# Memory keys and values as four weight stages, the values computed with tokens in partitions

## What is computed

```python
X_HEADS, X_HEAD_DIM, MEM_LEN = 4, 128, 256

def rmsnorm(x, g):
    return x * lax.rsqrt(jnp.mean(x * x, axis=-1, keepdims=True) + NORM_EPS) * g

def memory_cross_attn(xq, mem_kv):          # mem_kv = rmsnorm(memory, g) @ w_mem_kv[layer]: 256 x 1024
    q = xq.reshape(bsz, t, X_HEADS, X_HEAD_DIM)
    k, v = jnp.split(mem_kv, 2, axis=-1)
    ...
    s = jnp.einsum('bthd,bmhd->bhtm', q, k) * (X_HEAD_DIM ** -0.5)
    p = jax.nn.softmax(s, axis=-1)
    o = jnp.einsum('bhtm,bmhd->bthd', p, v)
```

## Time and profile before

| | |
|---|---|
| median of 3 runs | 2449.39 us (2448.02 to 2449.98) |
| the profiled execution, its time | 2450.39 us |
| its span, which the rows show | 2448.6 us |
| share of PE, PEld, DVE, ACT, POOL | 97%, 80%, 50%, 27%, 60% |
| mean clock granted to TensorE | 0.993 of full speed |

### The profile page before, as it was taken

How to read it: one execution, slowest core, us unless ns; L and a number is a source line. 1 busy time by engine, 2 the same in 40 slices (tenths; PEclk the granted TensorE clock), 3 DMA queues, 4 the chain that set the end, 5 groups by cost and what they waited for, 6 DMA issues and landing times.

```text
span 2448.6 us, 32730 instructions
## 1 busy us (share of the span) xinstructions
PE 2384.1 (97%) x12156; PEld 1964.8 (80%) x12156; DVE 1217.8 (50%) x2000; ACT 657.0 (27%) x1329; POOL 1457.1 (60%) x1461
## 2 busy tenths in 40 slices
PE   8999999999999999999999999999999989999997
PEld 6877778887888888787788888888888877888885
DVE  4335654334302325776358552055787874755402
ACT  3233321002201113455221110025666543111100
POOL 8654456666666667554458777661333355877761
PEclk9999999999999999999999999999999999999998
DMA  4222222222222322221222222222112212222221
GB/s 171 90 95 87 87 77 96 95 95 95 95 95 95 123 99 88 70 87 53 69 86 95 95 96 96 101 78 69 54 68 70 70 52 78 95 95 95 97 99 54
DMA packets 59762, 214.49 MB, mean 88 GB/s; under 512 B 6624, under 2 KB 6752, under 8 KB 59488
## 3 DMA queue, kind: packets, MB, share of 16 engines
q1 hardware_dynamic: 56880, 206.55, 24.9%
q10 hardware_dynamic: 2736, 5.96, 0.7%
HBM read 210.38 MB, written 2.10 MB: 87 GB/s over the span
## 4 chain that ended last, share of the span: by engine, by line
PE 84%; DVE 11%; ACT 3%; issue 1%; DMA 0%; POOL 0%; DVEq 0%; ACTq 0%; POOLq 0%
PE acc L556 23%; PE acc L558 23%; PE acc L557 22%; PE ps_s L699 3%; PE ps_o L727 2%; PE ps_t L713 2%; PE acc L768 1%; PE acc L770 1%; PE acc L769 1%; DVE hg_in L2085 1%; DVE hg_in L1633 1%; ACT w_hi L1462 1%; DVE hg_level_q L2133 1%; DVE hg_level_k L2133 1%; DVE ps_s L1589 1%
## 5 line engine op out<-in xcount | busy, mean ns | idle before, releaser
L513 POOL CAST w_hi<-w_raw 128x512 fp32r<-128x512 f32 x688 | 439.9, 668 | 714.8 <-DMA w_raw<-stream 714.6
L556 PE MATMUL acc<-h_hi,w_hi 128*128 128x512 f32 (+1 forms) x1844 | 723.0, 392 | 6.4 <-DVE h_lo L1555 2.9
L558 PE MATMUL acc<-h_hi,w_lo 128*128 128x512 f32 (+1 forms) x1844 | 706.2, 383 | 0.0
L557 PE MATMUL acc<-h_lo,w_hi 128*128 128x512 f32 (+1 forms) x1844 | 704.8, 382 | 0.0
L515 POOL TENSOR_TENSOR w_lo<-w_raw,w_hi 128x512 fp32r<-128x512 f32 x384 | 514.2, 1339 | 231.2 <-ACT w_hi L1462 231.2
L517 POOL TENSOR_TENSOR w_lo<-w_raw,w_hi 128x512 fp32r<-128x512 f32 x384 | 532.7, 1387 | 0.0
L556 PEld LDWEIGHTS acc<-h_hi,w_hi 128*128 128x128 f32 x1844 | 347.7, 189 | 73.7 <-DVE h_lo L1555 4.7
L558 PEld LDWEIGHTS acc<-h_hi,w_lo 128*128 128x128 f32 x1844 | 346.9, 188 | 69.4
L557 PEld LDWEIGHTS acc<-h_lo,w_hi 128*128 128x128 f32 x1844 | 347.8, 189 | 64.0 <-issue 0.5
L1611 DVE COPY y_all<-acc 128x512 f32<-128x512 f32 x31 | 21.4, 691 | 270.0 <-PE acc L558 238.5
L556 PE MATMUL acc<-hid_hi,w_hi 128*128 128x512 f32 x352 | 138.9, 395 | 0.0
(11 more groups left out here) (346 smaller groups left out, 3685.6 us busy)
## 6 DMA issues: line engine op xcount, KB each, us to landing
w_raw<-stream SPq DMA_DIRECT2D x384, 512.0 KB, 3.2
toeplitz<-ext_in ACTq DMA_DIRECT2D x16, 256.0 KB, 3.7
out<-x_res SPq DMA_DIRECT2D x4, 512.0 KB, 2.6
x_res<-x_in SPq DMA_DIRECT2D x3, 512.0 KB, 7.0
mem<-mem_in ACTq DMA_DIRECT2D x1, 1024.0 KB, 5.5
consts<-consts_in SPq DMA_DIRECT2D x1, 656.0 KB, 9.6
x_res<-x_in SPq DMA_DIRECT2D x2, 256.0 KB, 5.1
rope<-rope_in ACTq DMA_DIRECT2D x1, 512.0 KB, 6.6
```

The lines of the kernel that those rows point to most:

```text
L513: nc.gpsimd.tensor_copy(hi[:, half], raw[:, half]).then_inc(hi_made, 1)
L556: nc.tensor.matmul(ps, hi, x_hi[:, k, 0:cols], start=(k == 0), stop=False)
L557: nc.tensor.matmul(ps, hi, x_lo[:, k, 0:cols], start=False, stop=False)
L558: mm = nc.tensor.matmul(ps, lo, x_hi[:, k, 0:cols], start=False, stop=(k == st.kt - 1))
```

## The change

`memkv` becomes four stages: `memk0`, `memv0`, `memk1`, `memv1`, each four column blocks of eight tiles. The stream holds the same tiles; those of `memv0` and `memv1` are now in the lead order, four tiles of one feature tile side by side. The keys are computed as before (`memk0` by the lead steps in units 9 to 16, `memk1` in 13 units). The values are computed as the first stages of the kernel do it: a block of 128 memory tokens is stationary, and the 512 value columns of the layer are moving, in 16 steps of three matmuls spread over 12 units. Two banks hold a layer's values, one for each token block, tokens in partitions, and ScalarE copies each of them to `mem_v` with the scale 1/rms of its token, which now lies along the partitions. The eight turnings, VectorE's eight scaled copies to `normed` and its eight copies out of `ps_t` are gone. For the new scale, `both_norms` computes two more columns: VectorE first adds the two halves of `mem_sq` (one more addition of 128x256), one 256-column product gives the row as before, and two one-column products, with `mem_sq` stationary, give the sums with tokens in partitions. Root and reciprocal cover 258 columns where they covered 256.

```diff
+MEMORY = ["memk0", "memv0", "memk1", "memv1"]
-LEAD = {*TOKENS, "up0", "memkv", "a_in", ...
+LEAD = {*TOKENS, "up0", "memk0", "memv0", "memv1", "a_in", ...
-    ("a_in", 16, 8), ("memkv", 16, 8), ("a_out", 8, 12), ...
+    ("a_in", 16, 8), *[(name, BANKS, 8) for name in MEMORY], ("a_out", 8, 12), ...
...
-        for c in range(st.cbs):
+        for c in range(MEM // P if name.startswith("memv") else st.cbs):
...
+        mem_part = [("memv0", 12), ("memk1", 13), ("memv1", 12)]
+        mem_at = {name: MEM_FIRST + sum(units for _, units in mem_part[:i]) for i, (name, _) in enumerate(mem_part)}
+        mem_at["a_out"] = MEM_FIRST + sum(units for _, units in mem_part)
...
-                    for half in range(2):
-                        mm = nc.tensor.matmul(ps_t[:, 0:MEM], const("ones"), mem_sq[:, 0, half * MEM:(half + 1) * MEM],
-                                              start=(half == 0), stop=(half == 1))
+                    nc.tensor.matmul(ps_t[:, 0:MEM], const("ones"), mem_sq[:, 0, 0:MEM], start=True, stop=True)
+                    for b in range(MEM // P):
+                        mm = nc.tensor.matmul(ps_t[:, MEM + b:MEM + b + 1], mem_sq[:, 0, b * P:(b + 1) * P], const("ones")[:, 0:1],
+                                              start=True, stop=True)
...
+            def mem_values(st, first, end):
+                for i in range(first, end):
+                    k, b = divmod(i, MEM // P)
+                    slot = st.first_slot + k // 2
+                    if k == 0:
+                        bank_free(st, b)
+                    if k % 2 == 0 and b == 0:
+                        pe.wait_ge(split_made, slot + 1)
+                    hi, lo = (w[:, slot % RING, BANKS * (k % 2):BANKS * (k % 2 + 1), :].rearrange("p t n -> p (t n)") for w in (w_hi, w_lo))
+                    out_, cols = banks[st.banks[b]][:], slice(b * P, (b + 1) * P)
+                    nc.tensor.matmul(out_, h_hi[:, k, cols], hi, start=(k == 0), stop=False)
+                    nc.tensor.matmul(out_, h_lo[:, k, cols], hi, start=False, stop=False)
+                    mm = nc.tensor.matmul(out_, h_hi[:, k, cols], lo, start=False, stop=(k == st.kt - 1))
+                    if k % 2 and b == MEM // P - 1:
+                        mm.then_inc(slot_done, 1)
...
-            for c in range(BANKS, mem_st.cbs):
-                if c % 8 >= 4:
-                    also[mem_turn(c) + 1].append(lambda c=c: transpose_v(mem_st, c, normed[:, c % 2, :], MEM // P))
...
+            def take_memory(layer):
+                st_ = stages[f"memv{layer}"]
+                act.wait_ge(slot_done, st_.first_slot + st_.slots)
+                for b in range(MEM // P):
+                    nc.scalar.activation(mem_v[layer][:, b, :], banks[st_.banks[b]][:], ACT.Copy,
+                                         scale=small["rstd_mem"][:, MEM + b:MEM + b + 1]).then_inc(st_.free, 1)
...
+            also[mem_at["memk1"]] = lambda: take_memory(0)
+            also[mem_at["a_out"]] = lambda: take_memory(1)
...
+            step.wait()
+            step(nc.vector.tensor_tensor(mem_sq[:, 0, 0:MEM], mem_sq[:, 0, 0:MEM], mem_sq[:, 0, MEM:], ALU.add), x_total)
```

More of the change, by code:

```diff
@@ L59 @@
 WIDE = {"ffn_in0": (4, 5, 6), "ffn_in1": (4, 5, 6), "b_in": (6, 5), "b_out": (4,)}
-LEAD = {*TOKENS, "up0", "memkv", "a_in", "a_out", "ffn_in0", "b_in", "b_out", "ffn_in1"}
+MEMORY = ["memk0", "memv0", "memk1", "memv1"]
+LEAD = {*TOKENS, "up0", "memk0", "memv0", "memv1", "a_in", "a_out", "ffn_in0", "b_in", "b_out", "ffn_in1"}
 STAGES = [
@@ L63 @@
     ("up0", HALF, 8), ("down0", 8, HALF), ("up1", HALF, 8), ("down1", 8, HALF),
-    ("a_in", 16, 8), ("memkv", 16, 8), ("a_out", 8, 12), ("ffn_in0", 2 * FF2, 8), ("ffn_out0", 8, FF2),
+    ("a_in", 16, 8), *[(name, BANKS, 8) for name in MEMORY], ("a_out", 8, 12), ("ffn_in0", 2 * FF2, 8), ("ffn_out0", 8, FF2),
     ("b_in", 44, 8), ("b_out", 8, 12), ("ffn_in1", 2 * FF2, 8), ("ffn_out1", 8, FF2),
@@ L932, in _ @@
                 also[MEM_LEAD[k]].append(lambda k=k: mem_lead(k))
-            for c in range(BANKS, mem_st.cbs):
-                if c % 8 >= 4:
-                    also[mem_turn(c) + 1].append(lambda c=c: transpose_v(mem_st, c, normed[:, c % 2, :], MEM // P))
-            for i in range(MEM_UNITS):
-                first, end = BANKS * DT + mem_cut[i], BANKS * DT + mem_cut[i + 1]
-                also[MEM_FIRST + i].append(lambda first=first, end=end: block_tiles(mem_st, first, end, h_hi, h_lo, MEM))
+            for name, units in mem_part:
+                steps = BANKS * DT if name == "memk1" else DT * MEM // P
+                for i in range(units):
+                    first, end = steps * i // units, steps * (i + 1) // units
+                    if name == "memk1":
+                        also[mem_at[name] + i].append(lambda first=first, end=end: block_tiles(stages["memk1"], first, end, h_hi, h_lo, MEM))
+                    else:
+                        also[mem_at[name] + i].append(lambda name=name, first=first, end=end: mem_values(stages[name], first, end))
             def mem_ready():
                 pe.wait_ge(stages["a_in"].free, stages["a_in"].cbs)
-                pe.wait_ge(mem_st.free, mem_st.cbs)
+                for name in MEMORY:
+                    pe.wait_ge(stages[name].free, len(stages[name].banks))
             also[X_FIRST - 2 * LOOK - 1].append(mem_ready)
@@ L1366, in _ @@
             n["x"] += DT
-            root(n["x"] // DT, 1.0 / D, small["eps_d"][:], MEM, summed=x_summed)
+            root(n["x"] // DT, 1.0 / D, small["eps_d"][:], MEM + 2, summed=x_summed)
             quarter, st = HEAD_DIM // 2, stages["a_in"]
@@ L1395, in _ @@
             st = stages["b_in"]
-            v0 = 8 + 2
+            v0 = 2
             def head_act(h, j, func, done):
@@ L2007, in _ @@
                 also[MEM_INPUT + i // 2].append(lambda i=i: mem_rest(i))
-            for c in range(mem_st.cbs):
-                also[MEM_FIRST + c // 2 - 1 if c < BANKS else mem_turn(c)].append(lambda c=c: mem_block(c))
-                if c >= BANKS:
-                    also[mem_turn(c) + 1].append(lambda c=c: mem_tokens(c))
+            for layer, at in enumerate((MEM_FIRST - 1, mem_at["memk1"])):
+                for c in range(BANKS):
+                    turn_ = at + c // 2 if layer == 0 else at + next(
+                        i for i in range(13) if BANKS * DT * (i + 1) // 13 >= (c + 1) * DT) + 1
+                    also[turn_].append(lambda layer=layer, c=c: scaled(stages[f"memk{layer}"], c, mem_k[layer][:, c, :],
+                                                                       rstd_of=small["rstd_mem"]))
             first_o = n["o"]
```

22 lines of the change are left out of this document (4 added, 18 removed).

## The result

The kernel became slower, not faster. Its median is **2454.81 us** (2452.85 to 2456.7) against 2449.39 us before: a ratio of 1.0021, with a 95% interval of 1.0014 to 1.0027, so 5.4 us more. The forecast was 2441.6 us, in a range that ended at 2445.5. The profiled execution took 2454.98 us, 4.59 us more than that of the kernel before, at nearly the same granted clock (0.992 against 0.993).

The account below looks back on a forecast made before the run. TensorE was taken as the bound, its largest wait being value turnings held by ScalarE's copy out of ps_t. 7.0 + 0 + 0 + 1.0 - 0.1 - 0.1 = 7.8 us saved from 2449.39: 2441.6 us, range 2439.0 to 2445.5.

Parts of the forecast that it names:

- Smaller edits: Slots, VectorE's copies, additional sum, norm products, wider root and reciprocal, short units: 0.1 us lost in norm, 0.1 in units.
- signs of being wrong: Filled-stretch waits of turn or weigh above 2 us, granted clock below 1.00 there, or gain shown there and lost later.
- The turnings: Seven value-block turnings in the filled attention stretch go, each 0.91 to 1.07 us: 7.0 us saved, counted in full.
- Rival (b): Filled stretch: the wait is handed on and 4.3 us returns as waits of turn; 2445.9 us, chance 0.10.
- rival (c): TensorE's clock falls in 1141 to 1156 us, costing up to 12.4 us more; 2454.0 us, chance 0.05.
- ScalarE's copies: Turns 30 and 55: two 128x512 copies each, 0.59 us per copy; taken as 0 in turn 30, net 0 at tail.
- cover of "0.1 to 0.5 us": Turn 30: ScalarE free at about 2.8 us, TensorE needs take about 3.3 us after; cost 0, at most 1.2 us.
- rival (a): ScalarE's four copies come through to TensorE, up to 2.4 us, plus 0.5 for short units; 2444.5 us, chance 0.08.
- The eighth turning: Unit 56, without fill: ScalarE's copy 0.22 us earlier; net with new copies a 0.3 loss to 0.7 gain, taken as 0.
- The products: Memory values: 192 matmuls of 256 columns become 96 of 512, 0.227 us against 0.238 for two: 1.0 us saved.
- rival (d): Value products among attention units run slower, say 0.24 us: 1.2 us plus 1.0 not gained; 2443.8 us, chance 0.05.
- The norm products: Memory norm before a_in: two 256-column and two one-column products' passes, 0.78 against 0.67 us: 0.1 us lost, called real.

Follow-up runs that it names:

- spread copies: Changed kernel, arena 128 bytes higher, ScalarE's value copies one to a turn (31, 33, 55, 57) instead of two in turns 30 and 55: 2435.94 us, ratio 0.9947.
- arena held: Changed kernel with the arena at its old address, root_warm sharing the bytes of eps_q: 2444.87 us, ratio 0.9983 to the kernel before.
- + 192: Kernel before with only its arena moved 192 bytes higher: 2442.69 us, ratio 0.9969.
- + 64: Kernel before with only its arena moved 64 bytes higher: 2459.94 us, ratio 1.0042.
- + 128: Kernel before with only its arena moved 128 bytes higher: 2460.22 us, ratio 1.0042.

## Why the prediction was wrong, step by step

**The step that failed is a term in "Smaller edits"**: "Two more columns in root and reciprocal: nothing that shows". As work on ScalarE and VectorE they are indeed nothing (ratio 1.0002 alone). But I did not follow the two columns through the allocation. They move every tile of the arena by 64 bytes, and that costs 9.9 us (10.2 in the kernel before), more than the whole gain. None of my rivals was of this kind. The stretches that lost the time were not edited, so a part-by-part costing could not reach them, and the range was too narrow on that side. Of the signs of being wrong that the prediction lists, one came: the gain shows in the stretch and is lost elsewhere, a part of it before the stretch.

**The turnings: right.** Forecast 7.0 us for seven, measured 6.9 in the attention stretch, and 7.2 and 6.1 by medians (eighth included). The turnings stood in units 23, 26, 29, 32, 47, 50, 53 and 56. In units 22 and 23, where the first one stood, the changed kernel has new products behind each `turn` and no wait:

```profile
1070.09 0.44 PE L715 MATMUL ps_t<-consts,probs 128*128 128x128 f32 x2
1070.28 0.47 PE L939 MATMUL acc<-w_hi,h_hi 128*128 128x512 f32 x1
...
1071.06 0.38 PE L715 MATMUL ps_t<-consts,probs 128*128 128x128 f32 x2
1071.19 0.48 PE L939 MATMUL acc<-w_hi,h_hi 128*128 128x512 f32 x1
1071.51 0.39 PE L940 MATMUL acc<-w_hi,h_lo 128*128 128x512 f32 x1
...
1072.44 0.40 PE L941 MATMUL acc<-w_lo,h_hi 128*128 128x512 f32 x1
```

The distance from `turn` to product is 0.13 us in unit 23, where it was 1.16, and 0.13 to 0.30 us in all 37 units, as forecast; the 4.3 us of the earlier trace rows are gone. Rival (b), the wait handed on, happened for 1.0 us of the 4.3 at most: what TensorE waits for from 1043 to 1160 us is now

```profile
PE ps_t L715 <- ACT probs_t L1231: 3.0, 5, 0.9
PE ps_o L729 <- ACT probs_t L1231: 0.8, 2, 0.5
```

3.8 us in all. Before it was the 4.3 us of the earlier trace rows and, in the same view,

```profile
PE ps_t L713 <- ACT probs_t L1210: 2.1, 4, 0.6
PE ps_t L713 <- DVE mem_v L1650: 0.5, 1, 0.5
```

so 6.9 us. The 4.3 and 0.5 us at the turnings are gone, and the other waits grew from 2.1 to 3.8: by 1.0 in the kernel that only leaves the turnings out as well (3.1 us there), and by 0.7 behind the copies, below. Only 0.3 us of the 3.8 lies in the stretch filled with products, 1048 to 1137 us. By stretch, against the earlier trace rows, TensorE is fuller in both, and the clock stays at 1.00, so rival (c) did not happen either:

```profile
1141.00:1156.00 15.00, 12.89 (x105) 10.50 (x105) 11.23 (x39) 8.97 (x30) 1.96 (x2) 1.00 0.00 1
1043.00:1142.00 99.00, 96.84 (x879) 78.37 (x878) 66.89 (x209) 61.81 (x208) 58.22 (x64) 1.00 0.26 86
```

**ScalarE's copies: mis-sized.** I priced one at 0.59 us by the copy of `ps_o` and took no cost in turn 30 and a net of 0 at the tail. One took 676 ns:

```profile
L1412 ACT ACTIVATE mem_v<-acc,rstd_mem 128x512 f32<-128x512 f32 x4 | 2.5, 676 | 0.0
```

In turn 30 the cover of "0.1 to 0.5 us" was not there. ScalarE's two copies end at 1089.22, its copy of `probs_t` starts at 1089.11, and `weigh` waits for that:

```profile
1087.97 1.25 ACT L1412 ACTIVATE mem_v<-acc,rstd_mem 128x512 f32<-128x512 f32 x2
...
1089.64 0.66 PE L729 MATMUL ps_o<-probs_t,v_win 128*64 128x128 f32 x8 [0.26 <-ACT probs_t L1231]
```

In turn 55 the second `turn` and `weigh` of unit 56 both wait:

```profile
1137.16 1.25 ACT L1412 ACTIVATE mem_v<-acc,rstd_mem 128x512 f32<-128x512 f32 x2
...
1138.74 0.44 PE L715 MATMUL ps_t<-consts,probs 128*128 128x128 f32 x2 [0.85 <-ACT probs_t L1231]
...
1140.36 0.66 PE L729 MATMUL ps_o<-probs_t,v_win 128*64 128x128 f32 x8 [0.55 <-ACT probs_t L1231]
```

Moving the copies to VectorE gives back 0.3 us at the first place (the pair of units 30 and 31 takes 3.47 instead of 3.80 us) and 0.4 at the second (units 56 and 57, 3.13 instead of 3.51), and spreading them gives back the same 0.7. So rival (a) had the right mechanism and was worth 0.7 us, not 2.9. With the spread copies TensorE's waits from 1060 us are shorter:

```profile
PE ps_t L715 <- ACT probs_t L1231: 2.6, 5, 0.6
PE ps_o L729 <- ACT probs_t L1231: 0.5, 1, 0.5
```

**The eighth turning** is worth 0.3 us: the pair of units 56 and 57 takes 3.13 us instead of 3.47 (forecast 0.22).

**The products: right in sign, under half in size.** Forecast 1.0 us saved; with the copies out of the way (VectorE's version) the attention stretch takes 101.44 us, against 101.82 with the turnings alone removed. That is 0.4 us. The groups in the changed kernel:

```profile
L939 PE MATMUL acc<-w_hi,h_hi 128*128 128x512 f32 x32 | 14.6, 456 | 0.0
L941 PE MATMUL acc<-w_lo,h_hi 128*128 128x512 f32 x32 | 12.7, 396 | 0.0
L940 PE MATMUL acc<-w_hi,h_lo 128*128 128x512 f32 x32 | 12.5, 392 | 0.0
```

From 1071.51 to 1072.44 are four distances of 0.233 us (the rows above), which is also the median over all units with values, where I took 0.227 from the earlier trace rows. So rival (d), which supposed 0.24, was about half right: 96 x 0.006 = 0.6 us of the 1.0 is not gained, which leaves 0.4. Its price of 2.2 us was wrong besides, since the 1.2 us of slower products already holds the 1.0 not gained. An estimate by the Trainium skill, "TensorE: Matmul & The Clock Gate", section "Back-to-back issue gap", whose 2.5 ns per matmul are for an isolated one, is 0.24 us for 96 matmuls fewer; the measured saving is between that and my 1.0, and nearer to it.

These terms close the attention stretch: 6.9 + 0.3 - 0.7 + 0.4 = 6.9 us, and the changed kernel's stretch is 109.02 - 102.07 = 6.95 us shorter. The forecast for the same work was 7.9.

**The norm products**: forecast 0.1 us lost, measured nothing by medians (1.0002), within an interval that is much wider than the term. My reason for calling it real was wrong: the wait at the fifth block did not move when the chain of the reciprocal did.

**What stays open.** Placement held equal, the medians give the edit 4.9 us (arena held; 4.2 by the ratio, whose interval is 2.0 to 6.4), 4.3 (both at the weights' place) and 5.1 (both 64 bytes further up), while the profiled executions show 6.9 in the stretch and the turnings alone gave 7.2 and 6.1. The roughly 2 us between are within the intervals of some pairs and not of all. Spreading ScalarE's copies lowers the median by 2.4 us where the attention stretch shows 0.7, and the intervals overlap.

One candidate stands in the traces, before the first window score. `a_in` turns `v_feat` through `ps_t`, and in the profiled execution of the changed kernel at the weights' place TensorE waited there for VectorE, whose operations of 128x512 take anything from 0.69 to 1.67 us in that stage:

```profile
PE ps_t L686 <- DVE v_feat L1664: 2.9, 1, 2.9
```

Of the seven traces with the norm's edit, four have this wait (0.2 us in the other three), and of the eight without it none. It also explains most of what the spread copies seemed to gain: between those two profiled executions, 2439.01 and 2435.3 us, 2.6 us lie before the first window score and 0.7 in the attention stretch. Against it: taking the memory's reciprocal out of VectorE's way did not lower the median (2438.7 against 2437.83). With one trace of each kernel, how often the long wait comes is not shown.

The clock is another. In some executions a stretch at half clock near 1033 us lasts 6.8 us and in others 3.4, worth 1.7 us. The mean clocks listed for each execution average 0.9929 with the arena held and 0.9933 for the kernel before, about 1 us; but they are rounded to 0.001, 2.4 us, and count half clock at the very end too, where TensorE has no work left. This part is not settled.

## What to carry to other kernels

When an edit changes the size of any buffer, compute the address of every buffer behind it, and count that as a part of the change; to judge the edit itself, time it with all addresses held. If matmuls of unedited stages get longer at full clock and without idle time, look at the placement of their operands before looking at the edit; here putting the moving tile at the weights' place in 256 bytes was worth 7.1 us, as much as the whole edit. One profiled execution is no measure of a median: before a gain is put down to an edit, compare also the stretches that it does not touch. Work that an engine has time for on average still has to be cut into pieces no longer than its slack in the one turn where it stands.

## What the runs showed of the hardware

I had not expected the distance of matmuls (512 columns, a new 128x128 weight load before each, full clock) to depend on where the moving operand starts against the stationary one, modulo 256 bytes in a partition:

| moving tile against the stationary one | mean distance, three kinds (ns) | from |
|---|---|---|
| same place | 226.5, 226.5, 227.0 | kernel before, `+ 192` |
| 64 bytes further | 231.7, 226.0, 229.1 | kernel before |
| 128 further | 233.2, 233.5, 233.3 | kernel before, `+ 64` |
| 192 further | 233.4, 233.6, 233.0 | kernel before, `+ 128` |

A shift of all tiles together changes nothing (231.7, 225.8, 229.3). It is up to 3% of a matmul's distance. It holds too where the weights are what moves: with `h` 64 bytes up, the moving weights lie 192 further than the stationary `h`, and the token stages have 233.1 to 233.4 ns, as in the last row. The four places are 64 bytes apart; nothing between them was tried, and other sizes and types of matmul were not measured. What inside the chip causes it, no run here shows; the runs show the dependence only.
